# Old SSD states go through the second norm pair of PSUM, and ScalarE copies them

## What is computed

```python
# D_INNER = 2048, 32 heads of 64, 4 groups of 8 heads, D_STATE = 128, DEC_BATCH = 8, DEC_SEQ = 16
states = jnp.einsum('bcsgn,bcges,bcsgep->bcgepn', Bm, decay_states, xd)
states = jnp.concatenate([h0.reshape(nb, G, E, P, N)[:, None], states], axis=1)
new_states = jnp.einsum('bgezc,bcgepn->bzgepn', decay_chunk, states)
states_in, final = new_states[:, :-1], new_states[:, -1]
y_off = jnp.einsum('bclgn,bcgepn,bcgel->bclgep', Cm, states_in, jnp.exp(A_cs))
y = (y_diag + y_off).reshape(nb, L, SSD_HEADS, P)
y = y + p['ssd_D'].astype(jnp.float32)[:, None] * xs_h
y = y.reshape(nb, L, D_INNER).astype(u.dtype) * jax.nn.silu(z)
y = _rmsnorm(y.reshape(nb, L, SSD_GROUPS, D_INNER // SSD_GROUPS), ...)
```

## Time and profile before

| | us |
|---|---|
| median of 3 runs (lowest, highest) | 1973.6 (1973.21, 1981.63) |
| profiled execution, its own time | 1978.57 |
| its span, first to last instruction | 1977.0 |
| TensorE busy | 1918.2 (97%) |
| VectorE busy | 1078.0 (55%) |
| ScalarE busy | 725.0 (37%) |
| mean granted clock of TensorE over the span | 0.974 |

### The profile page before, as it was taken

How to read it: one execution, slowest core, us unless ns; L and a number is a source line. 1 busy time by engine, 2 the same in 40 slices (tenths; PEclk the granted TensorE clock), 3 DMA queues, 4 the chain that set the end, 5 groups by cost and what they waited for, 6 DMA issues and landing times.

```text
span 1977.0 us, 31917 instructions
## 1 busy us (share of the span) xinstructions
PE 1918.2 (97%) x12877; PEld 1859.4 (94%) x12877; DVE 1078.0 (55%) x1355; ACT 725.0 (37%) x1141; POOL 113.0 (6%) x219
## 2 busy tenths in 40 slices
PE   8999999998899999999999999998799999999998
PEld 7999999998799999989998998987799999999998
DVE  6442443345687654566577677666745433442444
ACT  5221332223477644334545444542333221221222
POOL 2000000000012100001011010100000000000000
PEclk9999999999899999999998998997899999999999
DMA  4222222222222242334224323322622222222222
GB/s 140 74 70 75 68 83 73 76 67 84 91 72 74 72 119 86 95 98 124 78 70 113 103 78 111 96 69 78 224 76 65 74 75 76 74 76 76 75 66 77
DMA packets 268066, 171.68 MB, mean 87 GB/s; under 512 B 6534, under 2 KB 259642, under 8 KB 267677
## 3 DMA queue, kind: packets, MB, share of 16 engines
q1 hardware_dynamic: 239840, 129.52, 22.8%
q0 software_dynamic: 7072, 26.34, 4.3%
q10 hardware_dynamic: 21072, 14.69, 2.3%
HBM read 150.03 MB, written 20.48 MB: 86 GB/s over the span
## 4 chain that ended last, share of the span: by engine, by line
PE 85%; DVE 7%; ACT 3%; issue 2%; DMA 1%; DVEq 0%; ACTq 0%
PE pu L635 76%; PE pu L901 1%; DMA merged<-gate_spill 1%; PE pn L830 1%; PE pn L889 1%; ACT w_hi L977 1%; PE pn L858 1%; PE pn L840 1%; DVE h_t L1786 1%; PE pn L862 1%; DVE w_lo L1343 1%; DVE bc L1337 1%; DVE squares L1337 1%; PE pu L692 0%; DVE h_a L1793 0%
## 5 line engine op out<-in xcount | busy, mean ns | idle before, releaser
L1343 DVE TENSOR_TENSOR w_lo<-w_raw,w_hi 128x1024 fp32r<-128x1024 f32 x240 | 295.7, 1232 | 503.1 <-ACT w_hi L977 501.2
L635 PE MATMUL pu<-act_hi,w_hi 128*128 128x320 f32 x2336 | 542.3, 313 | 12.2 <-ACT act_hi L1004 7.4
L635 PE MATMUL pu<-act_lo,w_hi 128*128 128x320 f32 x2336 | 534.8, 310 | 2.1 <-DVE act_lo L1384 2.0
L635 PE MATMUL pu<-act_hi,w_lo 128*128 128x320 f32 x2336 | 534.0, 310 | 0.0
L977 ACT ACTIVATE w_hi<-w_raw 128x1024 fp32r<-128x1024 f32 x240 | 253.6, 1057 | 536.6 <-PE pu L635 532.9
L635 PEld LDWEIGHTS pu<-act_hi,w_hi 128*128 128x128 f32 x2336 | 394.4, 189 | 28.0 <-issue 21.0
L635 PEld LDWEIGHTS pu<-act_lo,w_hi 128*128 128x128 f32 x2336 | 391.9, 189 | 3.5 <-DVE act_lo L1384 3.1
L635 PEld LDWEIGHTS pu<-act_hi,w_lo 128*128 128x128 f32 x2336 | 392.8, 189 | 0.0
L635 PE MATMUL pu<-h_hi,w_hi 128*128 128x320 f32 x1056 | 241.7, 310 | 0.7 <-DVE ff_g L1401 0.7
L635 PE MATMUL pu<-h_lo,w_hi 128*128 128x320 f32 x1056 | 241.5, 310 | 0.0
L635 PE MATMUL pu<-h_hi,w_lo 128*128 128x320 f32 x1056 | 241.0, 309 | 0.0
(11 more groups left out here) (319 smaller groups left out, 1980.0 us busy)
## 6 DMA issues: line engine op xcount, KB each, us to landing
w_raw<-in_ffn_w_up_dram SPq DMA_DIRECT2D x87, 512.0 KB, 3.8
w_raw<-in_w_in_dram SPq DMA_DIRECT2D x73, 512.0 KB, 3.9
w_raw<-in_ffn_w_down_dram SPq DMA_DIRECT2D x32, 512.0 KB, 3.8
w_raw<-in_w_br_ssd_dram SPq DMA_DIRECT2D x16, 512.0 KB, 3.4
w_raw<-in_ffn_w_down_dram SPq DMA_DIRECT2D x16, 384.0 KB, 3.4
es<-e_spill POOLq DMA_DIRECT2D x40, 128.0 KB, 2.9
merged<-gate_spill POOLq DMA_DIRECT2D x8, 640.0 KB, 5.3
h_a<-in_state_ssd_h_dram POOLq DMA_DIRECT2D x8, 512.0 KB, 6.3
```

The costliest lines, as they stand in the source:

```text
L635: ins = pe.matmul(dst[:, h, :], w[:, side, c, :], a[:, k, h * HALF:(h + 1) * HALF], start=(at == 0), stop=(at == n - 1))
L1343: dve.tensor_tensor(w_lo[:, side, :, :], w_raw[:, side, :, :], w_hi[:, side, :, :].bitcast(F32), ALU.subtract).then_inc(s["w_lo_done"], 1)
```

## The change

The old states leave `pu`. Their transposes go into `pn[1]`, one head pair at a time (`old_state`), and ScalarE copies each from there into its half of `h0_t` (`old_copy`) with the new semaphores `old_mm` and `old_cp`. Only the first one, (0,0), stands ahead of `inner`, the other three behind the middle unit, where transposes and contributions alternate. `new_state(0,0)` moves between the contributions (1,0) and (1,1). ScalarE makes the copies (0,1), (1,0), (1,1) behind the prompt's squares and ahead of the middle unit, or, without a middle unit, all four ahead of the squares. VectorE loses its four copies; both `decay_states` move behind the middle unit's taps and ahead of its silu and `new_states(0)`; without a middle unit the squares' sums go behind `new_states(0)`. The four outputs a group of `old` are gone from the numbering, which keeps its parity. A parameter `amid` is added to `products` and `unit`, which no caller uses. The diff, without `amid`:

```diff
@@ -79,10 +79,8 @@
                 yield name, 1, 2 if name[0] == "br" else 1
         for name in sampled_unit:
             yield name, 1, 1
-        yield ("old", g, 0), 0, 2
         for name in middle:
             yield name, 1, 1
-        yield ("old", g, 1), 0, 2
         yield ("new", g, 0), 0, 2
         yield ("new", g, 1), 0, 2
         for name in after:
@@ -142,7 +140,7 @@
 sq_clear sq_done sq_part sq_added sq_summed ln_ready rs_act rs_step xn_done xh_done xl_done ff_th ff_s ff_hi ff_lo start_v start_a g1_in w_part0 w_part1 w_part2 w_part_hi w_part_lo g1_mm g1_cp hist_mm vec_mm
 hist_in ext_in conv tail_in wg_in gates_mm lru_v lru_a htail_in spill e_out es_in0 es_in1 yl_hi_done yl_lo_done
 dt_v dt_a dt_p gtr xb_th xb_out z_th m_built ht_zero ssd_p ssd_a ssd_v bseq
-h0_in0 h0_in1 hs_step hs_out0 hs_out1 hp_mm hp_cp hp_out yz yn_hi_done yn_lo_done br_s gl_th gl_out0 gl_out1 gs_th gs_out
+h0_in0 h0_in1 hs_step old_mm old_cp hs_out0 hs_out1 hp_mm hp_cp hp_out yz yn_hi_done yn_lo_done br_s gl_th gl_out0 gl_out1 gs_th gs_out
 ma_in0 ma_in1 mg_b mg_v mh_done ml_done reload tail_mm tail_cp tails_out gfin fin_a fin_v y_a y_v y_dma""".split()
 
 
@@ -869,51 +869,57 @@
                                        ht[:, 2 * q:2 * q + 2, :].rearrange("n a b -> n (a b)"), ident[:, :])
                 ins.then_inc(s["hp_mm"], 1)
 
-                def old_states(qq):
-
+                def old_state(qq, a):
+
+                    n = g * 4 + 2 * qq + a
                     pe.wait_ge(s[f"h0_in{qq}"], g * 32 + 32)
-                    for a in range(2):
-                        o = O_AT["old", g, qq] + a
-                        open_out(o)
-                        for b in range(DEC_B):
-                            ins = pe.transpose(pu[o % 2][:, b // 4, (b % 4) * P:(b % 4 + 1) * P], h0[qq][:, a, b, :], ident[:, :])
-                        ins.then_inc(s["out_ready"], 1)
-
-                def from_states(qq):
-
-                    for a in range(2):
-                        q = 2 * qq + a
-                        pe.wait_ge(s["out_free"], O_AT["old", g, qq] + a + 1)
-                        for b in range(DEC_B):
-                            c = SEQ + b * DEC_L
-                            ins = pe.matmul(pn[0][:, 1, q * P + b * DEC_L:q * P + (b + 1) * DEC_L], h0_t[:, a, b, :],
-                                            xft(g, 5)[:, c:c + DEC_L], start=True, stop=True)
+                    if qq or a:
+                        pe.wait_ge(s["old_cp"], n)
+                    else:
+                        pe.wait_ge(s["ssd_a"], g * SA * NT + SA * (NT - 1) + SA_L)
+                    for b in range(DEC_B):
+                        ins = pe.transpose(pn[1][:, b // 4, (b % 4) * P:(b % 4 + 1) * P], h0[qq][:, a, b, :], ident[:, :])
+                    ins.then_inc(s["old_mm"], 1)
+
+                def from_state(qq, a):
+
+                    q = 2 * qq + a
+                    pe.wait_ge(s["old_cp"], g * 4 + q + 1)
+                    for b in range(DEC_B):
+                        c = SEQ + b * DEC_L
+                        ins = pe.matmul(pn[0][:, 1, q * P + b * DEC_L:q * P + (b + 1) * DEC_L], h0_t[:, a, b, :],
+                                        xft(g, 5)[:, c:c + DEC_L], start=True, stop=True)
                     return ins
 
-                def new_states(qq):
-
-                    for a in range(2):
-                        o = O_AT["new", g, qq] + a
-                        open_out(o)
-                        q = 2 * qq + a
-                        for b in range(2):
-                            rows = slice(b * HD, (b + 1) * HD)
-                            ins = pe.matmul(pu[o % 2][:, b, :], xdd[rows, 2 * q:2 * q + 2, :].rearrange("p h d -> p (h d)"),
-                                            b_seq[rows, :, :].rearrange("p b n -> p (b n)"),
-                                            start=True, stop=True)
-                        ins.then_inc(s["out_ready"], 1)
+                def new_state(qq, a):
+
+                    o = O_AT["new", g, qq] + a
+                    open_out(o)
+                    q = 2 * qq + a
+                    for b in range(2):
+                        rows = slice(b * HD, (b + 1) * HD)
+                        ins = pe.matmul(pu[o % 2][:, b, :], xdd[rows, 2 * q:2 * q + 2, :].rearrange("p h d -> p (h d)"),
+                                        b_seq[rows, :, :].rearrange("p b n -> p (b n)"),
+                                        start=True, stop=True)
+                    ins.then_inc(s["out_ready"], 1)
 
                 scores(NT - 1)
                 fill(sampled_unit)
-                old_states(0)
+                old_state(0, 0)
                 inner(NT - 1)
                 fill(middle)
-                from_states(0)
-                old_states(1)
+                old_state(0, 1)
+                from_state(0, 0)
+                old_state(1, 0)
+                from_state(0, 1)
+                old_state(1, 1)
                 pe.wait_ge(s["bseq"], g + 1)
-                new_states(0)
-                from_states(1).then_inc(s["ssd_p"], 1)
-                new_states(1)
+                from_state(1, 0)
+                new_state(0, 0)
+                from_state(1, 1).then_inc(s["ssd_p"], 1)
+                new_state(0, 1)
+                new_state(1, 0)
+                new_state(1, 1)
                 fill(after)
 
             mix_unit(("gs", 6), act_hi, act_lo)
@@ -1264,10 +1270,32 @@
                     act.wait_ge(s["gl_out0"], 16 * 3)
                     act.wait_ge(s["gl_out1"], 16 * 2)
                 fill(sampled_unit)
-                for q in range(PAIRS):
+
+                def old_copy(qq, a):
+
+                    act.wait_ge(s["old_mm"], g * 4 + 2 * qq + a + 1)
+                    act.activation(h0_t[:, a, :, :].rearrange("p (c b) n -> p c (b n)", c=2), pn[1][:, :, :],
+                                   ACT.Copy).then_inc(s["old_cp"], 1)
+
+                def prompt_square(q):
+
                     act.wait_ge(s["yz"], g * SQG + q + 1)
                     square_tile(SQ_GRP + g * SQG + q, q % 2, xf[:, q, 0:SEQ])
-                fill(middle)
+
+                old_copy(0, 0)
+                if middle:
+                    for q in range(PAIRS):
+                        prompt_square(q)
+                    old_copy(0, 1)
+                    old_copy(1, 0)
+                    old_copy(1, 1)
+                    fill(middle)
+                else:
+                    old_copy(0, 1)
+                    old_copy(1, 0)
+                    old_copy(1, 1)
+                    for q in range(PAIRS):
+                        prompt_square(q)
 
                 for qq in range(2):
                     for a in range(2):
@@ -1778,16 +1806,9 @@
                     for name in held:
                         begin(name)
 
-                def old_states(qq):
-
-                    for a in range(2):
-                        o = O_AT["old", g, qq] + a
-                        dve.wait_ge(s["out_ready"], o + 1)
-                        dve.tensor_copy(h0_t[:, a, :, :].rearrange("p (c b) n -> p c (b n)", c=2),
-                                        pu[o % 2][:, :, :]).then_inc(s["out_free"], 1)
-
                 def decay_states(qq):
 
+                    dve.wait_ge(s["old_mm"], g * 4 + 2 * qq + 2)
                     for a in range(2):
                         dec = es[:, (NT - 1) % 2, 2 * qq + a, DEC_L - 1:P:DEC_L]
                         dve.tensor_tensor(h0[qq][:, a, :, :], h0[qq][:, a, :, :],
@@ -1805,25 +1826,25 @@
                 scores(NT - 1)
                 finish(held[0])
                 fill(sampled_unit)
-                sp_(NT - 1, SP_SEG)
-                old_states(0)
-                decay_in(NT - 1)
-                decay_states(0)
                 sv(NT - 2, SV_Y)
                 for q in range(PAIRS):
                     dve.tensor_tensor(xf[:, q, 0:SEQ], xf[:, q, 0:SEQ], sz[:, q, 0:SEQ], ALU.mult).then_inc(s["yz"], 1)
                 clear_sum(g + 1)
-                for q in range(PAIRS):
-                    add_square(SQ_GRP + g * SQG + q, q % 2, SEQ)
-                if middle and middle[0][0] == "xb":
+                decay_in(NT - 1)
+                if middle:
+                    for q in range(PAIRS):
+                        add_square(SQ_GRP + g * SQG + q, q % 2, SEQ)
                     xbc_taps(*middle[0][1:])
-                    old_states(1)
+                    decay_states(0)
+                    decay_states(1)
                     xbc_silu(*middle[0][1:])
+                    new_states(0)
                 else:
-                    fill(middle)
-                    old_states(1)
-                new_states(0)
-                decay_states(1)
+                    decay_states(0)
+                    decay_states(1)
+                    new_states(0)
+                    for q in range(PAIRS):
+                        add_square(SQ_GRP + g * SQG + q, q % 2, SEQ)
```

12 lines of the change are left out of this document (7 added, 5 removed).

## The result

| | before | after |
|---|---|---|
| median (lowest, highest), 6 runs each | 1973.12 (1971.36, 1981.63) | 1990.05 (1984.63, 1992.23) |
| ratio, 95% interval | | 1.0074 [1.0055, 1.0094] |
| profiled execution, its own time; its span | 1978.57; 1977.0 | 1991.87; 1990.3 |
| mean granted clock | 0.974 | 0.967 |

The change costs 16.9 us between the medians and 13.3 between the two spans; 1987.2 was predicted. The difference of the two differences is in the executions that the profiler took: that of before lay 5.5 us above its median, that of after 1.8.

A forecast was written before the change was run, and what follows sets the result against it. TensorE, busy 97% of the span, was taken as the bound. Groups 0 to 2 gave +6.4, +3.8 and +3.8 (+14.0 us), group 3 -0.4: +13.6 on the median 1973.6 is 1987.2 us, range 1974.5 to 1994.5.

The forecast's parts named there:

- Rival A: Behind the middle unit, VectorE's queue holds the last two new states, clock low: +13.6 us, 1987; chance 0.67.
- C: Behind the middle unit, VectorE isn't the limit, TensorE at low clock is: 1976.5 us; chance 0.08.
- D: At the group ends, TensorE runs without waits at 2.4 GHz: 1942 us; chance 0.05.
- B: At the group ends, transposes between the contributions keep 2.4 GHz: +0.9 us, 1974.5; chance 0.12.
- E: Behind the middle unit, the clock falls at the first contribution: +3.2 us in each group, 1997; chance 0.08.
- Its own signs: Profile after: ScalarE's cut 9 to 10 us behind the middle unit, third-new-state hole 2 to 8, groups 33 to 36.
- The front: First transpose to middle unit, groups 0 to 2: 2.14 us left, saving 1.8, 2.3 and 2.3 us.
- ScalarE's copies: Behind the middle unit: about 1.2 us each with start and return, under one contribution block of 1.74, costing nothing.
- The step on VectorE's queue: Groups 0 to 2, behind the last copy: third new state 12.1 us later, next weight unit 15.8 us later.
- When the last transpose ends: Groups 0 to 2: 8.5 us behind the middle unit; 6.6 if the clock never falls, 11.7 at the first contribution.
- Group 3: First transpose to gate unit: 29.2 us against 29.62, waits return as a wait for VectorE, -0.4 us.
- What follows the groups: Weight unit behind each group begins at low clock as before: no difference, bound 0 to 1 us each.

The follow-up runs named there:

- pair_ahead: Changed kernel with the transposes (0,1) back ahead of the middle unit in groups 0 to 2, their copy ahead of the squares; 1998.58 us, ratio 1.0097.
- decays_first: Changed kernel with both `decay_states` ahead of the middle unit's taps on VectorE in groups 0 to 2; 1976.83 us, ratio 1.0016.
- evac_between: Changed kernel with ScalarE's middle-unit weight cut between copies (0,1) and (1,0), its moves out of `pu` between (1,0) and (1,1); 1976.34 us, ratio 1.0015.
- grouped: Changed kernel with contributions (0,0) and (0,1) side by side, not alternating with transposes, behind the middle unit; 1996.62 us, ratio 1.0094.
- after_again: The changed kernel measured once more without an edit, beside other kernels on the same chip; 1988.53 us, ratio 1.0065.
- all_three: Changed kernel with decays_first and evac_between together, plus group 3's sums of squares ahead of its second decays; 1968.01 us, ratio 0.9968.
- no_queue: Changed kernel with ScalarE as in evac_between, group 3's sums early, and each VectorE call in groups 0 to 2 where its input comes; 1964.52 us, ratio 0.9937.
- amid_all: Changed kernel with three transposes and two contributions among the sampled unit's matmuls in all groups, and another VectorE order; 1967.2 us, ratio 0.9961.
- amid_g3: Changed kernel with three transposes and two contributions among the sampled unit's matmuls in group 3 alone; 1983.96 us, ratio 1.0046.

## Why the prediction was right, and where its steps were off

**Sign and size.** +13.6 was the sum, +13.3 lies between the spans and 16.9 between the medians. Rival A holds in its mechanism, the wait for VectorE's queue. C and D (VectorE not the limit, neither holds) fall by the holes in front of the third new state, B by the clock, which fell in every group, E by the 4.4 to 8.7 us of full clock after the first contribution in groups 0 to 2. But the closeness of 13.6 to 13.3 is luck: the groups 0 to 2 came out 7.0 us below their sum, group 3 came out 1.3 above it, and what lies outside the stretches, put at nothing, is 5.4. The four places themselves cost 7.9 us.

**Its own signs.** The copies, the front without a hole, the hole of 2 to 8 us in front of the third new state and the one at the gate came as written. Three signs failed: ScalarE's cut stands 7.2, 8.0 and 7.2 us behind M and not 9 to 10, the groups take 32.1 to 32.9 us and not 33 to 36, and the clock stayed at 1.00 past the fourth block behind M, which ends at M + 5.2 (in group 1 by only 0.1 us). The prediction had named the last as a sign of being wrong. All three are one error, the place of the clock's fall.

**The front** was 2.14 us by the sum and is 1.99: no hole, nothing on the list of waits for the copy. pair_ahead shows the saving by undoing it.

**ScalarE's copies** at 1.02 to 1.03 us, all under other work of TensorE but the first of group 3 (1.13 us of waiting, foreseen). Right.

**The step on VectorE's queue** was right to a few tenths: cut to third new state 11.9 against 12.1 us, cut to next weight unit 15.7 (1042.75 to 1058.47) against 15.8. decays_first and evac_between show each half of that chain to be a cause.

**When the last transpose ends** is the mis-sized term. The step put the clock's fall at M + 4.45, from the 3.9 and 2.9 us of before, where contributions stood side by side; here it came at M + 9.6, M + 5.3 and M + 7.3. So the last T ended at M + 6.1, M + 6.9 and M + 6.1 instead of M + 8.5, and the groups are 32.08, 32.90 and 32.08 instead of 34.7: 7.0 us too much for three groups. With the measured ends the same sum gives 9.14 + 6.1 + 1.1 + 15.7 = 32.0, and 32.8 for group 1. The rival that the transposes keep the clock has the earlier part on its side, with 1.00 until the last T had ended in groups 0 and 2, and is wrong in its end; whether it was the alternation that did it, no run shows (grouped and pair_ahead). The rule weighed there (the Trainium skill, "TensorE: Matmul & The Clock Gate", part 1: a busy TensorE has the full clock, idle gaps take it) does not describe it: the slices at 849 and 1040 show 0.50 with TensorE busy for the whole microsecond.

**Group 3** was 29.2 by the sum and is 30.51: the wait came back at the gate, ended by the addition into `h_b`, as written; the size is 1.3 us off, since the clock fell 5.8 us behind the first T and not 7.6 as the sum had it from before: the last two T start 5.8 and 10.8 us behind it instead of 5.9 and 9.8, and all that follows is late by about that.

**What follows the groups** was taken as no difference, 0 to 1 us each. It is +5.4 between the two profiles, of which the gate unit, at 0.70 of the clock instead of 0.89, is 1.8. It is TensorE at the lower clock, not a wait. Counted in slices of 1 us, TensorE works outside the four stretches for 34.7 us at the lower clock in before, 49.3 in after, 40.9 in after_again, 38.8 in decays_first and 29.0 in all_three, and the rest of the span is 1857.3, 1862.7, 1859.3, 1857.0 and 1854.4 us. Over the ten profiles of the table that is some 0.4 us of the rest for each such microsecond, to within 1.2 us, so by this estimate the 14.6 us more are worth all of the 5.4. Why the clock falls there oftener in one execution than in another stays open, and with it how much of this term belongs to the change. What is shown is that some 10 of the 13 us by after_again's ratio vanish with decays_first.

**The two bases.** I added a difference of spans to a median. The profiled execution of before was 5.5 us above its median and that of after 1.8, so 3.6 of the 16.9 us come from that step. The clock has a part in this too: beside after_again, 13 executions of before took 1971.4 to 1976.5 us with a mean clock of 0.976 to 0.979 and two took 1981.0 and 1982.4 with 0.975, and the profiled one has 0.974; so an execution at the median may well have shorter stretches than the ones shown. No trace shows one.

## What to carry to other kernels

Moving copies off the busier engine does not help if they then stand in front of the work for which that busier engine waits: follow the late item through both in-order queues up to the buffer that TensorE needs, before counting what TensorE saves. Then order each queue by when its inputs arrive; here two calls exchanged on VectorE, or the weight cut and the moves brought forward on ScalarE, were each worth some 10 us of 13, and the full reordering turned +0.7% into -0.6%. While a hole is on the path, clock and TensorE time hide in it; when it is closed they set the length.

## What the runs showed of the hardware

The granted clock falls to 0.50 under contributions of 16 columns with TensorE busy for 1.00 of each microsecond (slices 849:850 and 1040:1041). How soon it falls is not fixed by the order of the instructions: in groups 0 to 2 2.5 to 5.0 us after the first contribution side by side, 4.0 to 11.8 us alternated with transposes, 3.7 to 4.1 us in pair_ahead, which alternates too, and in group 3 1.0 to 1.7 us in six kernels that alternate and 8.9 to 9.2 in two. The same instruction order gives different places in different groups of one execution (9.0, 4.0 and 8.9 us in no_queue); why is open. Between the matmuls of a weight unit it did not fall: ten blocks of contributions in amid_all and amid_g3, all at 1.00.

The price is large for so short a stretch: 30.71 against 26.13 us for the same group, and 27.74 against 20.74 for group 3. The spread between executions of one kernel goes with it: in no_queue 1955.7 to 1958.4 us come with a mean clock of 0.980 to 0.982 and 1964.5 to 1969.0 with 0.975 to 0.977.
